# Conv layer of a diffusion step: opening by pairs of channel blocks, layer norm split in three parts

## The chip, the cores and the metric

The kernel runs on one core of a Trainium2 chip. The metric is the device time of one execution in microseconds (us), median of several runs. The core has a matrix engine (TensorE, in the profile PE, its weight loads PEld), a vector engine (VectorE, DVE), a scalar engine (ScalarE, ACT), GpSimd (POOL) and SyncE (SP), which here only issues DMAs. Each engine works through its own instruction list in order; engines are ordered among each other by semaphores alone, all written out by hand in this kernel.

## The reference, cut to what matters

One step of a two-layer backbone over T = 384 tokens: 128 context tokens (condition `c_ctx`) and 256 latent tokens (condition `c`). D = 1024, so there are 8 channel blocks of 128. Layer 0 mixes tokens with a convolution module; this case changes its opening and its layer norm. A dense SwiGLU, a latent attention layer and a mixture of 8 experts follow and are untouched.

```python
def adaln(cond, w, b):                       # w is D x 6D
    m = jax.nn.silu(cond) @ w + b
    return jnp.split(m[:, None, :], N_MOD, axis=-1)   # shift, scale, gate, shift, scale, gate

def conv_module(h, pw1, dw, dw_b, ln_g, ln_b, pw2):
    a, g = jnp.split(h @ pw1, 2, axis=-1)
    u = a * jax.nn.sigmoid(g)
    u = lax.conv_general_dilated(u, dw, ...31 taps, per channel...) + dw_b
    u = jax.nn.silu(layer_norm(u, ln_g, ln_b))
    return u @ pw2

# layer 0:  m = adaln(cond, ada_w[0], ada_b[0])
h = rms_norm(x, norm1_g[0]) * (1 + m[1]) + m[0]
x = x + m[2] * conv_module(h, ...)
```

## The kernel before, in words

**Weights.** All weights come through one ring of 6 slots of 1 MiB (`raw`, 128 x 2048 floats), numbered `s` and loaded by SP in that order; `load` makes SP wait until the chunk six places earlier has been read. Adaptive-norm chunks (`ada`) are used whole, in fp32: `cst` (the silu of both conditions, padded to 32 columns) is the stationary operand, four matmuls of 512 columns write four column groups of one PSUM bank, and eight chunks add up to one third of a layer's modulation. All other weights are split in two parts of lower width: ACT copies the chunk into `wh` (`make_hi`, L255), DVE subtracts it into `wl` (`make_lo`, L261), three buffers each (`HL`); a product is then three matmuls (`mm3`, L277 to L279). Activations are split the same way by DVE (`split_block`, L415 and L417).

**Opening.** SP loads three `ada` chunks, then x, then five more `ada` chunks; a chunk is 128 rows of ada_w, each 2048 columns and so 8 KB in one piece. These eight give shift and scale of the first norm for all channels. ACT squares x (L309), DVE takes the inverse root (`rsqrt`) and scales x into `xn` (L387), PE transposes `xn` block by block (`norm_pe`, L396). After the eighth chunk DVE adds the bias (`add_bias`, L1042), PE transposes the rows (`turn_rows`, L1650), DVE forms `modv` and `modA` (`modulation`), ACT applies them to each transposed block (L321), DVE splits it, and PE may start on it.

**Rounds.** `conv_pw1` comes in 8 chunks of 1 MiB (`PW1 + 3 r`; 1 KB pieces). Round r has 48 matmuls of 384 columns (two output blocks times 8 channel blocks times 3) and then two further `ada` chunks. Even rounds give two blocks of `a`, odd rounds the matching two of `g`; after each odd round ACT takes the sigmoid and DVE multiplies (`glu`, L1080). DVE carries the depthwise convolution of 6 of the 8 blocks, 31 taps each, 186 instructions (L1068, L1072); `ROUND_TAPS` says how many in which round, with `glu` and the `make_lo` of the next round's chunk ahead of them. ACT builds diagonal matrices (`diagonal`, L713), with which PE convolves the last two blocks after the rounds (L1697), between further `ada` chunks.

**Layer norm.** After the taps PE sums over channels with a matrix of ones (L1691), DVE centres the 8 blocks (L1123), ACT squares them, PE sums again (L1713). ACT takes one root over all 399 columns (L749), DVE one reciprocal (L1128), and then per block a scaling (L1132), a silu on ACT (L753) and the split. PE starts `conv_pw2` when block 0 is split for all tokens.

Of the kernel before, what the change touches and what calls it, by code (L numbers as in the profile page):

```python
# [53 lines left out]
def hybrid_conv_mla_diffusion_step(nc, d, out):  # L54
# [30 lines left out]
    PW1 = ADA_G  # L85
    ADA1 = PW1 + 3 * DK
# [20 lines left out]
    with ctx:  # L107
# [19 lines left out]
        vT = sb("vT", [P, 64])  # L127
# [62 lines left out]
        N1G, N2G, DWB, LNG, LNB, QNG, QKG, KKG = 0, 16, 32, 40, 48, 56, 62, 63  # L190
# [15 lines left out]
        kinds = [False] * ADA_G + [True, False, False] * DK + [False] * (2 * ADA_G) + [True] * 6 + [False] * DK  # L206
# [25 lines left out]

        def load(sp, s, src, view, loop=None):
# [16 lines left out]
        def make_hi(act, s, loop=None):  # L250

            turns = None if loop is None else (loop[0], loop[1] // RAW * 16)
            act.wait_ge(raw_in[s % RAW], at(16 * (s // RAW + 1), turns))
# [52 lines left out]
        def norm_act(act, q, layer, n, before_, count, banks=(6, 7) * 4, between=None, blocks=range(DK)):  # L306
# [8 lines left out]
            if layer == n == 0:  # L315
                make_hi(act, PW1)
            act.wait_ge(sem("mods"), 8 * layer + 4 * n + 4)
            for j in blocks:
                act.wait_ge(*of_norm(q, "turned", DK, j + 1))
# [7 lines left out]
        def norm_act_rows(act, q, layer, n, before_, banks, between=None):  # L327
# [16 lines left out]
            act.wait_ge(sem("mods"), 8 * layer + 4 * n + 4)  # L344
# [37 lines left out]
        def norm_dve(dve, step, q):  # L382
            dve.wait_ge(*of_norm(q, "squares", TC, TC))
            rsqrt(step, st[:, 4:4 + TC], st[:, 0:TC], TC)
            dve.sem_inc(sem("rstd"), 1)
            for c in (0, 2):
# [15 lines left out]
        CONV_BANKS = (2, 3, 6, 7, 0, 1, 6, 7)  # L402
        ADA_BANKS = ((5, 4), (6, 6), (7, 7), (2, 2), (6, 7), (0, 1))
        FFN_BANKS = (2, 3, 4, 5) * 2
        MODS_MADE = (4, 6, 8, 12, 14, 16)
# [6 lines left out]
        def split_block(dve, q, made, per, j):  # L412

            dve.wait_ge(sem(made), per * (j + 1))
# [16 lines left out]
        def _(sp):  # L431
# [5 lines left out]
            for n in range(ADA_G):  # L437
                if n == 3:
                    sp.dma_start(x[:, 0, :], d["x_prompt"][0]).then_inc(sem("x_in"), 16)
                    sp.dma_start(x[:, 1:3, :], d["x_sample"][0].rearrange("(c p) n -> p c n", p=P)).then_inc(sem("x_in"), 16)  # L440
                load_ada(n, 0, n)
            for r in range(DK):
                load(sp, PW1 + 3 * r, rows(d["conv_pw1"][0], 0, DK, r % 2 * D + r // 2 * 256, 256), as_rows(256, DK))
                for i in range(2):
                    load_ada(PW1 + 3 * r + 1 + i, 0, ADA_G + 2 * r + i)
# [94 lines left out]
        def _(pool):  # L540
# [8 lines left out]
            pool.memset(u[:, :, :], 0.0).then_inc(sem("zeroed"), 1)  # L549

            def fetch_bias(layer):
                b = d["ada_b"][layer].rearrange("(g j n) -> j g n", g=3, j=4)
                for j in range(4):
                    pool.dma_start(ab[32 * j:32 * j + 2, :, :], b[j].partition_broadcast(2)).then_inc(sem(f"bias_in{layer}"), 16)

            def keep_gate(layer, which):
                q = 3 * layer + 1 + which
                pool.wait_ge(sem("rows_added"), q + 1)
# [12 lines left out]
            fetch_bias(0)  # L571
# [3 lines left out]
            fetch_bias(1)  # L575
# [13 lines left out]
            pool.wait_ge(sem("mods"), 16)  # L589
# [101 lines left out]
        def _(act):  # L691
# [7 lines left out]
            for n, name in ((N1G, "norm1_g"), (N2G, "norm2_g"), (DWB, "conv_dw_b"), (LNG, "conv_ln_g"), (LNB, "conv_ln_b"),  # L699
                            (QNG, "mla_q_norm_g"), (QNG + 4, "mla_kv_norm_g")):  # L700
                vrow(n, d[name].rearrange("a (k p) -> (a k) p", p=P))
            vrow(QKG, d["mla_q_qk_g"][0:1, 0:P])
# [19 lines left out]
            for r in range(DK):  # L722
                if r + 1 < DK:
                    make_hi(act, PW1 + 3 * (r + 1))
                for n in range(3 * r, 3 * r + 3):
                    diagonal(n)
                if r % 2 == 1:
                    t = r // 2
                    act.wait_ge(chunk_used, used(PW1 + 3 * r))
# [1493 lines left out]
```

## Time and profile before

| | us |
|---|---|
| median of 3 runs | 1437.97 (1437.23 to 1440.47) |
| the profiled execution, its own time | 1436.74 |
| its span in the trace | 1435.0 |
| PE busy | 1366.1 |
| DVE busy | 1060.5 |
| ACT busy | 756.0 |
| DMA, mean over the span | 245 GB/s |

Span times run from the first instruction in the trace; 1.7 us lie around the span. PE is busy for 95% of it, but the share differs by stage, and the stages that the change touches are the first 238 us.

### The profile page before, as it was taken

Reading aid. Unit: us, or ns where it says so; the run is one execution under the profiler, and the core shown is the slowest. Engines: PE = TensorE matmul, PEld = TensorE weight load, DVE = VectorE, ACT = ScalarE, POOL = GpSimd, SP = SyncE. Lnnn points to the kernel's source line nnn. Section 1 sums busy time; section 2 is a strip of 40 time slices with the busy share of each in tenths; the row PEclk is TensorE's granted clock in tenths of the full one; section 3 lists DMA queues with packets and bytes.
Section 4 is the critical chain, followed back from the end, with each engine's and each line's share of the span. In section 5 each row is a group of like instructions: output and inputs, shape, how many; then the busy total and the mean of one; then the engine's idle time right before and its main releaser. Section 6 shows DMA issues by size and latency. Waiting matters only on the chain.

```text
span 1435.0 us, 18715 instructions
## 1 busy us (share of the span) xinstructions
PE 1366.1 (95%) x6686; PEld 1098.8 (77%) x6687; DVE 1060.5 (74%) x1328; ACT 756.0 (53%) x764; POOL 104.4 (7%) x129
## 2 busy tenths in 40 slices
PE   4999989999999989899999988999999999999997
PEld 1885457899999978677777766888878878778875
DVE  2589995443343447888888888888888888888986
ACT  2421354331322345655565545777777777777773
POOL 2000000401000000100000004500000000000003
PEclk8999999999999999999999998999999999999999
DMA  9898656999843323322212324999999999999994
GB/s 376 293 335 318 224 185 225 396 368 69 188 140 100 98 88 101 109 93 67 66 66 92 111 92 159 422 357 388 368 362 395 369 363 395 371 361 385 381 359 154
DMA packets 91914, 351.17 MB, mean 245 GB/s; under 512 B 7279, under 2 KB 43447, under 8 KB 62679
## 3 DMA queue, kind: packets, MB, share of 16 engines
q1 hardware_dynamic: 81088, 316.95, 61.7%
q0 software_dynamic: 9040, 28.66, 5.8%
q10 hardware_dynamic: 1735, 4.89, 0.9%
q8 instruction: 30, 0.49, 0.1%
q14 instruction: 21, 0.17, 0.0%
HBM read 326.13 MB, written 24.35 MB: 244 GB/s over the span
## 4 chain that ended last, share of the span: by engine, by line
PE 82%; DVE 8%; ACT 4%; issue 3%; DMA 2%; ACTq 0%; POOL 0%; DVEq 0%; POOLq 0%
PE ps L277 23%; PE ps L279 22%; PE ps L278 22%; PE ps L1697 3%; PE ps L1642 3%; DVE wl L261 2%; DVE hm L1549 2%; PE ps L1943 2%; PE ps L1974 2%; DMA raw<-in_conv_pw 1%; ACT wh L255 1%; PE ps L1947 1%; PE ps L2105 1%; PE ps L2064 1%; ACT QB L850 0%
## 5 line engine op out<-in xcount | busy, mean ns | idle before, releaser
L261 DVE TENSOR_TENSOR wl<-raw,wh 128x2048 fp32r<-128x2048 f32 x253 | 575.8, 2290 | 146.5 <-ACT wh L255 146.2
L255 ACT ACTIVATE wh<-raw 128x2048 fp32r<-128x2048 f32 x253 | 484.1, 1917 | 302.4 <-PE ps L279 260.4
L277 PE MATMUL ps<-wh,xgh 128*128 128x512 f32 x432 | 173.6, 402 | 0.2 <-DVE wl L261 0.2
L279 PE MATMUL ps<-wh,xgl 128*128 128x512 f32 x432 | 171.2, 396 | 0.0
L278 PE MATMUL ps<-wl,xgh 128*128 128x512 f32 x432 | 171.0, 396 | 0.0
L277 PE MATMUL ps<-hTh,wh 128*128 128x384 f32 x480 | 164.9, 344 | 1.8 <-DVE hTl L417 1.8
L278 PE MATMUL ps<-hTl,wh 128*128 128x384 f32 x480 | 163.5, 341 | 0.0
L279 PE MATMUL ps<-hTh,wl 128*128 128x384 f32 x480 | 163.2, 340 | 0.0
L277 PE MATMUL ps<-wh,hgh 128*128 128x512 f32 x288 | 116.3, 404 | 4.6 <-DVE hgl L1555 1.9
L279 PE MATMUL ps<-wh,hgl 128*128 128x512 f32 x288 | 114.1, 396 | 0.0
L278 PE MATMUL ps<-wl,hgh 128*128 128x512 f32 x288 | 114.1, 396 | 0.0
L1072 DVE SCALAR_TENSOR_TENSOR v<-u,dwT,v 128x399 f32<-128x399 f32 x180 | 99.0, 624 | 0.0
L277 PEld LDWEIGHTS ps<-hTh,wh 128*128 128x128 f32 x480 | 90.8, 189 | 10.5 <-issue 8.1
L279 PEld LDWEIGHTS ps<-wh,xgl 128*128 128x128 f32 x432 | 81.4, 188 | 19.8
L1156 DVE TENSOR_TENSOR ff<-ps,fs 128x384 f32<-128x384 f32 x22 | 12.3, 557 | 113.9 <-PE ps L279 113.9
L277 PEld LDWEIGHTS ps<-wh,xgh 128*128 128x128 f32 x432 | 81.4, 188 | 19.2 <-DVE wl L261 0.4
L278 PEld LDWEIGHTS ps<-wl,xgh 128*128 128x128 f32 x432 | 81.4, 188 | 18.2
L278 PEld LDWEIGHTS ps<-hTl,wh 128*128 128x128 f32 x480 | 90.8, 189 | 0.4
L279 PEld LDWEIGHTS ps<-hTh,wl 128*128 128x128 f32 x480 | 90.8, 189 | 0.0
L277 PEld LDWEIGHTS ps<-wh,hgh 128*128 128x128 f32 x288 | 54.2, 188 | 21.9 <-DVE wl L261 6.9
L279 PEld LDWEIGHTS ps<-wh,hgl 128*128 128x128 f32 x288 | 54.2, 188 | 13.1
L278 PEld LDWEIGHTS ps<-wl,hgh 128*128 128x128 f32 x288 | 54.3, 189 | 12.2
(368 smaller groups left out, 2127.4 us busy)
## 6 DMA issues: line engine op xcount, KB each, us to landing
raw<-in_moe_w SPq DMA_DIRECT2D x180, 1024.0 KB, 6.4
raw<-in_ada_w SPq DMA_DIRECT2D x48, 1024.0 KB, 7.2
raw<-in_ffn_w SPq DMA_DIRECT2D x33, 1024.0 KB, 12.1
raw<-in_conv_pw SPq DMA_DIRECT2D x12, 1024.0 KB, 9.2
raw<-in_mla_wo SPq DMA_DIRECT2D x8, 1024.0 KB, 4.9
xs_dram<-hf POOLq DMA_DIRECT2D x14, 512.0 KB, 21.4
ys_dram<-hf POOLq DMA_DIRECT2D x14, 512.0 KB, 22.4
raw<-in_mla_wuq SPq DMA_DIRECT2D x8, 768.0 KB, 4.6
```

The lines of the kernel that those rows point to most:

```text
L255: act.activation(wh[:, split_no(s) % HL, :], raw[:, s % RAW, :], ACT.Copy).then_inc(hi_made, 1)
L261: eng.tensor_tensor(wl[:, split_no(s) % HL, :], raw[:, s % RAW, :], wh[:, split_no(s) % HL, :], ALU.subtract).then_inc(lo_made, 1)
L277: nc.tensor.matmul(out_, sh, mh, start=start, stop=False)
L278: nc.tensor.matmul(out_, sh, ml, start=False, stop=False)
L279: return nc.tensor.matmul(out_, sl, mh, start=False, stop=stop)
L1072: dve.scalar_tensor_tensor(out=v[:, j, :], in0=u[:, j, w:w + CV], scalar=dwT[:, w * DK + j:w * DK + j + 1], in1=v[:, j, :], op0=ALU.mult, ...
L1549: dve.tensor_tensor(hm[:, g, :].rearrange("p (j r) -> p r j", j=4), ps[:, 3 + g, :].rearrange("p (r j) -> p r j", j=4), ms[:, g, :].rearra ...
L1642: last = pe.matmul(ps[32 * j:32 * j + 32, ADA_BANKS[q][0], :], cst[:, k, :], raw[:, s % RAW, j * 512:(j + 1) * 512], start=k == 0, stop=k ...
L1697: pe.matmul(ps[:, i, 0:CV], diag[:, m % DIAGS, :], u[:, DVE_BLOCKS + i, w:w + CV], start=w == 0, stop=w == CW - 1).then_inc(sem("diag_used ...
L1943: pe.matmul(ps[:, 2 * h + c // 2, a:b], QB[:, h, c * P:(c + 1) * P], KT[:, h, k0:k1], start=True, stop=False)
L1947: last = pe.matmul(ps[:, 2 * h + c // 2, a:b], QB[r0:r1, 2, c * P:(c + 1) * P], KR[r0:r1, k0:k1], start=False, stop=True)
L1974: last = pe.matmul(ps[:, 3 + h, P:T], v_sb[:, i, k + 1, h, :], pT[:, h, 2 * P * k:2 * P * (k + 1)], start=k == 0, stop=k == 2)
```

## The change

It does these things:

- The chunks that open the kernel are cut otherwise. An opening `ada` chunk now holds, for four row blocks of ada_w, 256 columns of shift and the 256 matching columns of scale, 1 KB pieces, loaded by two DMAs. Two such chunks (a pair) give shift and scale of two channel blocks for both conditions. The matmuls of one chunk write four row groups of a bank, each a partial sum; the four are added when the rows are turned, by a matmul against `folded_in`, a sum of four slices of the identity.
- Order of loads: x first, then pair 0, one `conv_pw1` chunk, pairs 1 and 2, one `conv_pw1` chunk, pair 3. The two `conv_pw1` chunks hold rows 0 to 511 and 512 to 1023 for two blocks of `a` and the two matching blocks of `g`; so the work of rounds 0 and 1 runs block by block (`open_block`, 12 matmuls each into four banks), two blocks per pair.
- The bias of this part comes transposed with the vectors (`ADB`, one more small DMA on ACT's queue).
- The 16 `ada` chunks of the rest of layer 0 lie in rounds 2 to 7: 3, 3, 3, 3, 2, 2 (before: two in each of 8 rounds). `add_bias(1)`, `turn_rows(1)` and `modulation(1)` come one round later.
- `ROUND_TAPS` has 78 taps in rounds 2 to 7, before 74.
- Layer norm: root, reciprocal, and for block 0 scaling, silu and split, run in three parts of 128, 143 and 128 columns; PE takes the first tokens of block 0 when the first part is split. `turn_rows(4)` comes after the second chunk of `conv_pw2`, before after the first.
- GpSimd fetches the bias for two thirds of layer 0 only and clears `u` after that.

```diff
+    QUARTERS = DK // 2
+    PAIR_BLOCKS = 4
+    OPEN = (0, 1, 3, 4, 5, 6, 8, 9)
+    ADA_ROUND = (0, 0, 3, 3, 3, 3, 2, 2)
+    PW1 = [2, 7] + [10 + r - 2 + sum(ADA_ROUND[:r]) for r in range(2, DK)]
-    ROUND_TAPS = (0, 0, 13, 13, 12, 12, 12, 12)
+    ROUND_TAPS = (0, 0, 14, 14, 13, 13, 12, 12)
+    LN_PARTS = ((0, P, 0), (P, SV + P, P), (SV + P, CV, 2 * P))
...
+            def load_pair(s, w, half, c0):
+                for t in range(2):
+                    load(sp, s, rows(w, 4 * half, 4, t * D + c0, 256),
+                         lambda slot: slot.rearrange("p (k t n) -> p k t n", k=4, t=2)[:, :, t, :])
...
+            def keep_rows(p):
+                dve.wait_ge(ada_used, 2 * (p + 1))
+                if p >= 2:
+                    dve.wait_ge(sem("rows_turned"), p - 1)
+                dve.tensor_copy(ar[:, p % 2, :], ps[:, p % 2, :]).then_inc(sem("rows_added"), 1)
...
-            norm_dve(dve, step, "conv")
+            norm_dve(dve, step, "conv", lambda: keep_rows(0))
...
+            modulation_pair(0)
+            for p in range(QUARTERS):
+                if p % 2 == 0:
+                    make_lo(dve, PW1[p // 2])
+                split_block(dve, "conv", "conv_modulated", 2, 2 * p)
+                split_block(dve, "conv", "conv_modulated", 2, 2 * p + 1)
+                if p + 1 < QUARTERS:
+                    keep_rows(p + 1)
+                    modulation_pair(p + 1)
...
+            ada_pair(0)
+            turn_vectors()
+            pe.wait_ge(sem("dw_made"), 3)
+            norm_pe(pe, "conv", CONV_BANKS, (0, 1))
+            turn_pair(0)
+            for p in range(QUARTERS):
+                if p + 1 < QUARTERS:
+                    ada_pair(p + 1, (0,))
+                    norm_pe(pe, "conv", CONV_BANKS, (2 * p + 2, 2 * p + 3))
+                if p % 2 == 0:
+                    wait_parts(pe, PW1[p // 2])
+                open_block(2 * p)
+                if p + 1 < QUARTERS:
+                    ada_pair(p + 1, (1,))
+                    turn_pair(p + 1)
+                open_block(2 * p + 1)
...
+            for i in range(TC + 1):
+                if i < TC:
+                    a, b, _ = LN_PARTS[i]
+                    dve.wait_ge(sem("ln_root"), i + 1)
+                    step(dve.reciprocal(rs[:, a:b], sd[:, a:b]))
+                else:
+                    dve.tensor_tensor(v[:, 1, :], v[:, 1, :], rs, ALU.mult).then_inc(sem("ln_scaled"), 1)
+                if i > 0:
+                    o = LN_PARTS[i - 1][2]
+                    dve.wait_ge(sem("ln_done"), i)
+                    high = dve.tensor_copy(hTh[:, 0, o:o + P], hf[:, 0, o:o + P])
...
+                    dve.tensor_tensor(hTl[:, 0, o:o + P], hf[:, 0, o:o + P], hTh[:, 0, o:o + P], ALU.subtract)\
+                        .then_inc(sem("ln_h_lo"), 1)
+                if i < TC:
+                    dve.tensor_tensor(v[:, 0, a:b], v[:, 0, a:b], rs[:, a:b], ALU.mult).then_inc(sem("ln_scaled"), 1)
```

## Rows read from the trace of the kernel before

**Rows 1.** Page, head and part 1: the span and the matrix engine's share.

```profile
span 1435.0 us, 18715 instructions
PE 1366.1 (95%) x6686; PEld 1098.8 (77%) x6687; DVE 1060.5 (74%) x1328; ACT 756.0 (53%) x764; POOL 104.4 (7%) x129
```

**Rows 2.** Stages: length, busy PE, PEld, DVE, ACT, POOL, PE clock, DMA share, GB/s.

```profile
0.00:37.00 37.00, 16.80 (x95) 5.58 (x96) 8.67 (x27) 11.46 (x20) 7.81 (x15) 0.83 0.97 375
60.40:124.00 63.60, 63.50 (x389) 53.29 (x389) 54.79 (x89) 16.43 (x26) 2.19 (x4) 1.00 0.85 314
124.00:187.50 63.50, 62.53 (x244) 28.01 (x244) 62.44 (x120) 16.87 (x42) 3.28 (x6) 1.00 0.66 233
187.50:201.70 14.20, 10.30 (x49) 3.31 (x49) 13.56 (x17) 9.49 (x16) 0.00 (x0) 1.00 0.51 173
```

**Rows 3.** Timeline of the opening: start, length, engine, line, operation, count [idle before].

```profile
15.93 1.06 ACT L309 ACTIVATE xn<-x 128x1024 f32<-128x1024 f32 x1 [8.21 <-DMA x<-in_x_sample]
18.45 1.93 PE L1642 MATMUL ps<-raw,cst 128*32 128x512 f32 x8 [6.26 <-DMA raw<-in_ada_w]
21.77 1.42 DVE L387 TENSOR_SCALAR xn<-x,st 128x1024 f32<-128x1024 f32 x2
30.22 0.69 DVE L1042 TENSOR_TENSOR ar<-ps,ab 128x512 f32<-128x512 f32 x1 [3.87 <-issue]
30.96 0.66 PE L1650 MATMUL ps<-ident,ar 128*128 128x128 f32 x4 [0.88 <-DVE ar L1042]
33.20 6.53 ACT L321 ACTIVATE hf<-ps,modv,modA 128x128 f32<-128x128 f32 x16
33.33 2.29 DVE L261 TENSOR_TENSOR wl<-raw,wh 128x2048 fp32r<-128x2048 f32 x1 [1.29 <-ACT wh L255]
35.53 0.35 DVE L415 CAST hTh<-hf 128x384 fp32r<-128x384 f32 x1
35.92 0.56 DVE L417 TENSOR_TENSOR hTl<-hf,hTh 128x384 fp32r<-128x384 f32 x1
```

**Rows 4.** Windows as in rows 2: first ada chunks moving, then a conv_pw1 chunk.

```profile
20.00:25.00 5.00, 3.90 (x20) 0.40 (x16) 2.76 (x11) 1.15 (x1) 0.00 (x0) 0.52 1.01 421
44.00:46.00 2.00, 2.00 (x13) 2.00 (x12) 1.34 (x1) 1.40 (x4) 0.00 (x0) 1.00 1.09 350
```

**Rows 5.** Chain of waits that ended last, two matmuls of 384 columns: start, length.

```profile
37.79 0.32 PE ps L278
42.66 0.18 PE ps L277
```

**Rows 6.** Timeline of rounds 1 to 3: adas of one round, a load, its copy, taps.

```profile
58.41 1.92 PE L1642 MATMUL ps<-raw,cst 128*32 128x512 f32 x16
60.83 0.38 SPq L240 DMA_DIRECT2D raw<-in_conv_pw  x1
70.37 1.92 ACT L255 ACTIVATE wh<-raw 128x2048 fp32r<-128x2048 f32 x1 [8.03 <-DMA raw<-in_conv_pw]
74.53 7.17 DVE L1072 SCALAR_TENSOR_TENSOR v<-u,dwT,v 128x399 f32<-128x399 f32 x13
```

**Rows 7.** Timeline: the last glu, and the last channel sum before the mean.

```profile
122.92 1.02 DVE L1080 TENSOR_TENSOR u<-ps,sg 128x256 f32<-128x256 f32 x2 [0.32 <-ACT sg L732]
186.49 0.51 PEld L1691 LDWEIGHTS ps<-v,ones 128*128 128x128 f32 x2 [0.16 <-DVE v L1072]
```

**Rows 8.** Timeline of the layer norm: root, reciprocal, silu, first matmul of conv_pw2.

```profile
195.68 0.59 ACT L749 ACTIVATE sg<-ps,epsc 128x399 f32<-128x399 f32 x1
196.31 2.65 DVE L1128 RECIPROCAL sg<-sg 128x399 f32<-128x399 f32 x1 [0.31 <-ACT sg L749]
199.60 3.62 ACT L753 ACTIVATE hf<-v,vT 128x128 f32<-128x128 f32 x8 [2.02 <-DVE v L1132]
201.72 0.47 PE L277 MATMUL ps<-wh,hTh 128*128 128x512 f32 x1 [3.65 <-DVE hTl L417]
```

**Rows 9.** Window as in rows 2: the matrix engine's clock after a wait.

```profile
35.00:36.00 1.00, 0.15 (x1) 0.18 (x2) 0.97 (x3) 1.00 (x4) 0.00 (x0) 0.50 0.94 352
```

More of the change, by code:

```diff
@@ L231, in ffn_chunk, with landed @@
             return GATE2 - 2 + n if n < 2 else FFN + n
+        def landed(s):
+            return 16 * (s // RAW + 1 + sum(o % RAW == s % RAW for o in range(min(s + 1, PW1[2]))))
         def load(sp, s, src, view, loop=None):
@@ L385, in norm_dve @@
             dve.sem_inc(sem("rstd"), 1)
+            between()
             for c in (0, 2):
@@ L1651, in turn_rows, with ada_pair @@
                 last.then_inc(sem("rows_turned"), 1)
-            for n in range(ADA_G):
-                ada(n, 0, n)
-                if n == 5:
-                    turn_vectors()
-                if n == 6:
-                    pe.wait_ge(sem("dw_made"), 3)
-                    norm_pe(pe, "conv", CONV_BANKS, range(6))
-            turn_rows(0)
-            norm_pe(pe, "conv", CONV_BANKS, range(6, DK))
-            for r in range(DK):
-                t, s = r // 2, PW1 + 3 * r
+            def ada_pair(p, halves=(0, 1)):
+                for half in halves:
+                    s = OPEN[2 * p + half]
+                    pe.wait_ge(raw_in[s % RAW], landed(s))
+                    for k in range(4):
+                        last = pe.matmul(ps[32 * k:32 * k + 32, p % 2, :], cst[:, 4 * half + k, :],
+                                         raw[:, s % RAW, k * 512:(k + 1) * 512], start=half == 0, stop=half == 1)
+                    last.then_inc(ada_used, 1)
@@ new lines, in turn_pair, with open_block @@
+            def turn_pair(p):
+                if p == 0:
+                    pe.wait_ge(sem("pair_fold"), 2)
+                pe.wait_ge(sem("rows_added"), p + 1)
+                for i in range(4):
+                    last = pe.matmul(ps[:, p % 2, 2 * i:2 * i + 2], ar[:, p % 2, i * P:(i + 1) * P], folded_in[:, :],
+                                     start=True, stop=True)
+                last.then_inc(sem("rows_turned"), 1)
+            def open_block(k):
+                pe.wait_ge(sem("conv_h_lo"), k + 1)
+                hi, lo = parts(PW1[k // 4], 512, 4)
+                for m in range(PAIR_BLOCKS):
+                    last = mm3(ps[:, 2 + m, 0:T], hi[:, k % 4, m * P:(m + 1) * P], lo[:, k % 4, m * P:(m + 1) * P],
+                               hTh[:, k, :], hTl[:, k, :], k == 0, k == DK - 1)
+                if k % 4 == 3:
+                    last.then_inc(chunk_used, 1)
@@ L1664, in _ @@
+            n_ada = ADA_G
+            for r in range(2, DK):
+                t, s = r // 2, PW1[r]
                 wait_parts(pe, s)
@@ L1677, in _ @@
                 last.then_inc(chunk_used, 1)
-                for i in range(2):
-                    ada(s + 1 + i, 0, ADA_G + 2 * r + i)
-                if r == 4:
+                for i in range(ADA_ROUND[r]):
+                    ada(s + 1 + i, 0, n_ada)
+                    n_ada += 1
+                if r == 5:
                     turn_rows(1)
@@ L1720, in pw2_block @@
                 k = 2 * q + i
-                pe.wait_ge(sem("ln_h_lo"), k + 1)
+                pe.wait_ge(sem("ln_h_lo"), c + 1 if k == 0 else TC + k)
                 for h in range(2):
```

158 lines of the change are left out of this document (89 added, 69 removed).

## The prediction

> **What bounds the kernel now.** I read the head of the page first: PE is busy for 95% of the span [rows 1], so a change can win only where PE is not busy, or is busy at its lower clock. Then I cut the first 238 us into stages with the view of windows [rows 2]. The reader should see four different things there. Up to 37 us PE is busy for less than half of the time and the DMA engines are full (share 0.97): the opening waits for bytes. From 60.4 to 124 (rounds 2 to 7) PE is busy all the time, DVE for 54.8 of 63.6 us. From 124 to 187.5 both are, 62.5 us each. From 187.5 to 201.7 PE lacks 3.9 us, while DVE is busy for 13.6 of 14.2: the layer norm waits for DVE. Whatever is won in one stage is kept only if DVE in the next can follow; that is the whole question here. The profiled execution took 1436.74 us, 1.2 below the median of 1437.97; I work with differences in its span and take them off the median.
>
> **Opening: when the bytes land.** The trace gives two rates: 421 GB/s while 8 KB pieces move, 350 GB/s while 1 KB pieces move [rows 4]. One MiB so takes 2.5 us in the one form and 3.0 us in the other. x landed at 15.9 us behind 3 MiB of chunks [rows 3]; 4.5 MiB at 2.5 us are 11.25, so 4.7 us lie before the stream and around it. The change puts x first (1.5 MiB, landed near 8.4) and makes all ten opening chunks of 1 KB pieces: chunk 0 lands at 11.4, chunk 1 at 14.4, then one each 3.0 us: the first conv_pw1 chunk (2) at 17.4, the last (9) at 38.4, the next conv_pw1 (10) at 41.4. Before, eight ada chunks and the first conv_pw1 chunk were there by 31.4. So the new order brings work earlier, but the whole of it later.
>
> The Trainium skill (DMA: Bandwidth & Descriptors, Specifications) states a minimum of 512 B for line rate. By that rule the 1 KB pieces would lose nothing and the result would be the small rival named below; the trace speaks against it.
>
> **Opening: the first block.** DVE has the norm's inverse root ready before 14.4, but the change then makes it wait in `keep_rows(0)` for pair 0, and the scaling of x (1.4 us, [rows 3]) is queued behind that wait, and behind that the copies of the vectors, the transposes on PE and the turn. With an ada chunk at the low clock (1.9 us for one, [rows 3]): pair done 16.3; kept 17.0 (0.69, as the bias addition); x scaled 18.5; vectors copied 19.1 (0.6, three small copies); blocks 0 and 1 transposed and the pair turned by 21.3 (0.3 to 0.66 for a turn, [rows 3]); modulation of the pair 0.6, so 21.9. Then DVE makes `wl` (2.2 in sequence) and splits block 0 (0.9 for both steps) [rows 3]: PE's first `open_block` starts near 25.0. Before, the first matmul of this kind came at 37.1.
>
> **Opening: the pace.** An `open_block` is 12 matmuls of 0.18 us, 2.1 us at the full clock, 3.8 us at the lower (0.32 each, [rows 5]). Per pair PE does two of them (4.2), two ada chunks (0.95 each, [rows 6]), six transposes (0.8), and in `turn_pair` it waits for `keep_rows`, for which DVE needs 0.75 with the hop, plus 0.4 for the turn itself. That is 8.2 us a pair against 7.5 us of DMA (two and a half chunks), so with these terms PE's own chain sets the pace. From 25.0: block 0, an ada chunk, keep, turn and block 1 are 6.4; two full pairs 16.4; the last two blocks 4.2: rounds 0 and 1 are done at 52.0. Round 2 needs the `wl` of chunk 10, for which ACT starts only when all eight blocks are split: the last split comes about 3.6 us after the last turn (45.7), then 1.9 and 2.3 us of hi and lo: **round 2 starts at 53.0 to 53.6**, taken as 53.0 (hops between engines could add half a microsecond). Before it started at 60.4 [rows 2, 6]. So 7.4 us are won at this point. The bounds: 47.7 if only the landing of chunk 9 counted (38.4, then 9.3 us from ada to `wl`), and 57 if blocks 0 and 1 and what lies between ran at the lower clock and every hop cost 0.2 more. Folding four partial sums costs four tiny matmuls in place of four transposes, nothing measurable; what hides the two extra DMA issues per chunk (0.38 each, [rows 6]) is the 3.0 us that a chunk needs.
>
> **Rounds: what is given back.** The four ada chunks that lay in rounds 0 and 1 now lie in rounds 2 to 5: 4 x 0.95 = 3.8 us on PE, which is busy there throughout. Round 7's matmuls end at 53.0 + 51 + 14 x 0.95 + 1 = 118.3, before 121.9. DVE is the nearer limit. In round r it must make the `wl` of chunk r+1 ahead of its taps, and that chunk comes later now: with four chunks a round and six slots, SP may load conv_pw1 chunk r+2 only when the second ada chunk of round r has been read. Before, its issue at 60.83 hung on round 1 for chunk 4, and ACT copied it from 70.4 on [rows 6]. Now chunk 4 hangs on round 2: matmuls done at 61.5, first ada read at 62.4, two chunks of 2.5 and 3.0 plus 2.4 us of latency (the 60.83 load with two ada chunks 1.3 us ahead of it needed 10.5 for 8.1 us of bytes), landed 70.4, copied 72.4. So DVE starts round 3's taps at nearly the same time as before, whatever was won ahead. From there: 72.4 + 2.2, 14 taps (0.545 each in a series, [rows 6]), glu 0.95; chunk 5 is copied one PE round (11.35) after chunk 4, at 83.8; + 2.2 + 13 taps; chunk 6 at 95.1; + 2.2, bias 0.6, 13 taps, glu, `wl` 2.2, 12 taps, 12 taps: DVE is through at **121.4**, against PE's 118.3. The last glu so starts at 121.4, before at 122.92 [rows 7]: **1.5 us of the 7.4 are left.** Loads for three-ada rounds fill 10.5 to 10.7 of 11.35 us; the `wl` for PE is ready 1.0 us before PE wants it.
>
> **After the rounds.** PE is bound by its diagonals and ada chunks and DVE by its taps, and they meet at 186.5, where PE waits 0.16 and just before it 0.29 us for taps [rows 7]. DVE has four taps less (2.2 us), PE nothing less: **0.4 us.**
>
> **Layer norm.** Now root 195.7, reciprocal to 199.0, scaling, silu, split, PE at 201.7 [rows 8]. In three parts: first root 0.35 us, reciprocal 2.65 x 128/399 plus a fixed part = 0.95, scaling 0.3: 197.35. ACT does two more roots and reloads its table (1.3) until 198.1, silu 0.45, DVE cast and subtraction 0.5: PE starts at 199.15. Part 2 is split at 200.9, part 3 at 202.15, block 1 at 204.0 (before about 202.9), then one block each 1.35 us against 4.2 on PE. At the full clock PE does each third in 1.4 us, waits a little, and stands at 204.0 for block 1; seven blocks of 4.23 and the rest as before end at 234.0, before 237.5. **3.5 us.** At the lower clock, as now in the first 4 us, it would be 2.6, which is the lower bound; the upper is 4.0. I take 3.5 because PE's pause shrinks from 3.65 to 1.1 us. `turn_rows(4)` keeps its 0.4 us; what waits behind `modulation(4)` on DVE is the `wl` of the fourth conv_pw2 chunk, ready near 220 and wanted at 225.
>
> **Sum.** 1.5 + 0.4 + 3.5 = 5.4 us. After 238 us PE is the bound again and everything shifts. 1437.97 - 5.4 = 1432.6.
>
> **Rivals.** First, *the opening runs at the pace of its bytes*: round 2 at 47.7, DVE through at 116.1; gain 6.8 + 0.4 + 3.5 = 10.7, 1427.3. For it speaks the full DMA share [rows 2], against it the 8.2 us chain a pair. Second, *late conv_pw1 chunks*: the loads of three-ada rounds have 6% of air. If each lands 2 us later than computed, PE loses 1 us every second round and DVE 3 us by the end; its 1.5 becomes -1.5: gain 2.4, 1435.6. For it: before, chunk 7 came late while the gate fetch shared the engines. Third, on the other side, *the clock stays low through the opening*. After its 4.2 us pause PE's clock stood at the lower level [rows 9], and stayed there until 41.7. The new opening has a pause before every turn and before block 0. Four blocks at the lower clock cost 4 x 1.7 us, the ada chunks and transposes among them 5: 12 us later, 1444.6. It decides the sign once more than 5.4 us are lost, about half of that stretch. Against it: from 19 us on PE's pauses are each under 1.5 us.
>
> Two small ones shift the first block. *Block 0 at the lower clock*: before it lie mostly transposes and pauses, and before this change the clock rose only 4.6 us after the first matmul of the block kind; 1.7 us more, 1434.3. The Trainium skill (TensorE: Matmul & The Clock Gate, Part 4) says that transposes do not count as activity for the clock, which is this case; the trace can't separate it. *1 KB pieces at 421 GB/s*: chunks 0 and 1 each land 0.5 us earlier, the end 1.0: 1431.6; the 350 GB/s of [rows 4] are against it. This is what the 512 B of the Trainium skill's DMA page would give.
>
> **Chances.** Forecast 0.36, block 0 at the lower clock 0.11, 1 KB pieces at full rate 0.04, bytes' pace 0.12, late chunks 0.25, low clock 0.09, something else 0.03. 2.9 us are 0.2%, about what a measurement of this kernel can tell from no change. Faster by more (below 1435.1): the forecast and the small ones nearly whole (0.46 of 0.51), bytes' pace, a quarter of the late chunks, 0.64. Within: 0.26. Slower: 0.10. The range takes in the first two rivals and the bounds of the layer norm: 1427 to 1438.5.
>
> **What would show it.** Opening right: first open matmul near 25, round 2 near 53, the clock at 2.4 GHz from block 1 on. Rounds: DVE idle for about 7.5 us before the `wl` of chunk 4 near 72, then PE waiting for the last glu near 121 to 122 (about 2.5 us). Layer norm: first conv_pw2 matmul 2.9 us after the first reciprocal's start (now 5.4), at the full clock. Wrong: a round 2 before 50 or after 56, or a wait of PE for `wl` in rounds 3 to 6.

## The result and the profile after

The changed kernel took 1424.47 us (median of four, 1421.14 to 1427.03), the kernel before 1437.65 in the runs beside it. The ratio is 0.9903, with a 95% interval of 0.9885 to 0.9922: 13.2 us faster. The forecast was 5.4 us faster, 1432.6, in a range of 1427.0 to 1438.5; the time lies 2.5 us below that range.

The profiled execution took 1427.03 us. Page, head and part 1, after, beside [rows 1]:

```profile
span 1425.3 us, 18840 instructions
PE 1356.0 (95%) x6715; PEld 1097.1 (77%) x6715; DVE 1064.8 (75%) x1350; ACT 756.0 (53%) x767; POOL 102.9 (7%) x129
```

The share of PE is the same 95%, but its sum fell by 10.1 us, with no fewer matmuls. That is the first hint: a change that removes waits shortens the span and leaves the sum. A window of 100 us late in the kernel, where the change touches no instruction, says it plainly (length, then busy time and count of PE, PEld, DVE, ACT, POOL, clock, DMA share, GB/s). Before:

```profile
1000.00:1100.00 100.00, 99.73 (x447) 80.16 (x446) 88.09 (x48) 72.77 (x45) 0.00 (x0) 1.00 0.96 372
```

After:

```profile
1000.00:1100.00 100.00, 99.40 (x454) 80.86 (x453) 89.14 (x49) 74.32 (x47) 0.00 (x0) 1.00 0.97 381
```

Both at the full clock, both with PE busy throughout, and 454 matmuls in place of 447. The timeline of PE at 1000 us shows the pace of single matmuls (start, length). Before:

```profile
999.99 0.40 PE L277 MATMUL ps<-wh,xgh 128*128 128x512 f32 x1
1000.22 0.39 PE L278 MATMUL ps<-wl,xgh 128*128 128x512 f32 x1
1000.46 0.39 PE L279 MATMUL ps<-wh,xgl 128*128 128x512 f32 x1
1000.69 0.40 PE L277 MATMUL ps<-wh,xgh 128*128 128x512 f32 x1
```

After:

```profile
999.91 0.39 PE L287 MATMUL ps<-wh,xgh 128*128 128x512 f32 x1
1000.14 0.39 PE L288 MATMUL ps<-wl,xgh 128*128 128x512 f32 x1
1000.37 0.39 PE L289 MATMUL ps<-wh,xgl 128*128 128x512 f32 x1
1000.59 0.39 PE L287 MATMUL ps<-wh,xgh 128*128 128x512 f32 x1
```

Three matmuls need 0.70 us before and 0.68 after. Lengths overlap and are rounded, so from here on I use the mean distance from start to start of neighbouring matmuls of one kind over the whole trace, called the *spacing*; distances above 0.26 us (0.2 us for 384 columns), where PE did or waited for something else, are left out. For the expert products (2160 matmuls: three rows of 432 and three of 288 in the groups by line) it is 234.1 ns before and 229.3 after. 2160 x 4.8 ns are 10.4 us.

What the forecast spoke of lies in the first 235 us. Timeline of PE after, the opening:

```profile
14.20 1.93 PE L1730 MATMUL ps<-raw,cst 128*32 128x512 f32 x8 [1.14 <-DMA raw<-in_ada_w]
18.81 1.54 PE L407 MATMUL ps<-ident,xn 128*128 128x128 f32 x6 [1.93 <-DVE vT L1137]
25.60 0.66 PE L287 MATMUL ps<-hTh,wh 128*128 128x384 f32 x1 [0.42 <-DVE hTl L428]
26.06 0.52 PE L288 MATMUL ps<-hTl,wh 128*128 128x384 f32 x1
26.38 0.52 PE L289 MATMUL ps<-hTh,wl 128*128 128x384 f32 x1
...
29.71 1.07 PE L1730 MATMUL ps<-raw,cst 128*32 128x512 f32 x8
31.61 1.05 PE L1740 MATMUL ps<-folded_in,ar 128*128 128x2 f32 x8 [0.82 <-DVE ar L1093]
32.52 0.42 PE L287 MATMUL ps<-hTh,wh 128*128 128x384 f32 x1
...
50.46 0.42 PE L287 MATMUL ps<-hTh,wh 128*128 128x384 f32 x1
...
58.34 0.44 PE L287 MATMUL ps<-hTh,wh 128*128 128x384 f32 x1 [0.78 <-DVE wl L271]
```

Block 0 starts at 25.60, but its matmuls stand 0.32 us apart, the pace of the lower clock in [rows 5]; from 32.5 on they stand 0.18 apart. The clock column of the windows does not show this:

```profile
25.60:29.60 4.00, 4.00 (x12) 3.67 (x12) 0.68 (x2) 0.00 (x0) 0.00 (x0) 1.00 1.10 349
```

It reads 1.00 from the start of this trace to 128.8 us. So the lower clock of block 0 is read from the distance of the matmuls alone. The row at 58.34 is round 2 (before, the same kind of row starts at 60.27; the prediction took 60.4).

Timeline after, from the fourth conv_pw1 chunk's issue to the first diagonals (answering [rows 6, 7]):

```profile
68.91 0.38 SPq L250 DMA_DIRECT2D raw<-in_conv_pw  x1
77.97 2.29 DVE L271 TENSOR_TENSOR wl<-raw,wh 128x2048 fp32r<-128x2048 f32 x1 [8.09 <-ACT wh L265]
126.67 1.01 DVE L1126 TENSOR_TENSOR u<-ps,sg 128x256 f32<-128x256 f32 x2
127.74 3.39 PE L1806 MATMUL ps<-u,diag 128*128 128x399 f32 x6 [2.72 <-DVE u L1126]
```

And the layer norm after (answering [rows 8]):

```profile
193.06 3.93 DVE L1178 SCALAR_TENSOR_TENSOR v<-ps,v 128x399 f32<-128x399 f32 x8 [5.17 <-PE ps L1800]
201.53 0.95 DVE L1187 RECIPROCAL sg<-sg 128x128 f32<-128x128 f32 x1 [0.15 <-ACT sg L774]
204.57 0.47 PE L287 MATMUL ps<-wh,hTh 128*128 128x512 f32 x1 [1.12 <-DVE hTl L1199]
```

The wait of PE before conv_pw2 fell from 3.65 to 1.12 us. Behind it the clock stays full, where before it stood at 0.50 from 202.3 on:

```profile
202.30:205.70 3.40, 3.40 (x10) 2.63 (x9) 3.30 (x9) 2.82 (x7) 0.00 (x0) 0.50 1.10 351
```

Yet the first row of the conv layer's last step comes late. Timeline of DVE, before:

```profile
233.47 1.22 DVE L364 TENSOR_TENSOR xn<-ps,gate 128x1024 f32<-128x1024 f32 x1
```

After:

```profile
234.87 1.22 DVE L374 TENSOR_TENSOR xn<-ps,gate 128x1024 f32<-128x1024 f32 x1
```

I call this row the *end of conv*. From it to the end of the span the kernel before needs 1201.5 us and the changed one 1190.4. So the part that was rebuilt lost 1.4 us in these executions, and the part in which no instruction differs won 11.1.

### The profile page after: what moved, and what is told of

It is laid out like the page before. It is cut to its first block, busy times and chain, and to the rows that moved or that the text cites. A ratio compares the mean times of both kernels' runs of the same rounds, so it can differ in the third digit from the quotient of the medians.

```text
span 1425.3 us, 18840 instructions
## 1 busy us (share of the span) xinstructions
PE 1356.0 (95%) x6715; PEld 1097.1 (77%) x6715; DVE 1064.8 (75%) x1350; ACT 756.0 (53%) x767; POOL 102.9 (7%) x129
## 4 chain that ended last, share of the span: by engine, by line
PE 73%; DVE 11%; DMA 5%; ACT 4%; issue 4%; DVEq 0%; POOL 0%; ACTq 0%; SPq 0%; POOLq 0%
PE ps L287 20%; PE ps L289 19%; PE ps L288 19%; DMA raw<-in_ffn_w 3%; PE ps L1806 3%; DVE wl L271 3%; PE ps L1713 2%; DVE hm L1622 2%; PE ps L2052 2%; ACT wh L265 2%; PE ps L2083 2%; DVE v L1118 1%; PE ps L2056 1%; PE ps L2214 1%; PE ps L2173 1%
## 5 line engine op out<-in xcount | busy, mean ns | idle before, releaser
L288 PEld LDWEIGHTS ps<-wl,hgh 128*128 128x128 f32 x288 | 54.1, 188 | 11.1
```

The costliest lines, as they stand in the source:

```text
L288: nc.tensor.matmul(out_, sh, ml, start=False, stop=False)
```

## The experiments

**What could make untouched matmuls faster.** The full diff has one edit that reaches them (the excerpt above leaves it out): `vT` grows from 64 to 80 columns (64 bytes of each partition) and `folded_in`, 2 columns, comes behind it. Every tile allocated later moves, among them `hTh`, `xgh`, `hgh`, `ckTh`, `fh`, `oTh`; `raw`, `wh` and `wl` lie ahead of it and stay. In an expert product the moving operand is `wh` or `wl` and the stationary one `xgh` or `xgl`; in conv_pw1 `hTh` is moving and `wh` stationary. The theory: this move alone makes the gain. The rival: the gain comes from the new instructions (another rhythm of DMAs or of the clock after the conv layer).

The first set crosses the two. `e1_before_shifted` moves the tiles of the kernel before:

```diff
         vT = sb("vT", [P, 64])
+        spare = sb("spare", [P, 16])
+        spare2 = sb("spare2", [P, 2])
```

> The kernel before, with only two unused tiles of 16 and 2 columns put behind vT, so that every tile allocated after it lies where the changed kernel has it; no instruction differs. In the two traces the first 240 us of the changed kernel end 1.4 us later (first xn<-ps,gate at 234.87 against 233.47), and yet it is 13 us faster: the matmuls of 512 columns follow each other every 229.3 ns instead of 234.1. Theory A (the tiles' place in memory sets that spacing): this kernel is at about 1427, with 229 ns. Theory B (the spacing comes from what the new opening or layer norm does to the engines' timing or clock): it stays at 1437 to 1438 with 234 ns.

Measured: 1424.32 us, ratio 0.9899 (0.9883 to 0.9916), spacing 229.2 ns. The clock is not what made it faster: the granted clock as a mean over the profiled execution was 0.981, and 0.982 in that of the kernel before. The same window of 100 us:

```profile
1000.00:1100.00 100.00, 99.43 (x454) 81.05 (x453) 89.19 (x49) 74.21 (x47) 0.00 (x0) 1.00 0.97 382
```

The move acts on the conv layer too: the end of conv comes at 230.85 in e1, 2.6 us earlier than before.

`e2_after_unshifted` is the opposite, the changed kernel with its tiles back:

```diff
-        vT = sb("vT", [P, 80])
-        folded_in = sb("folded_in", [P, 2])
+        spare = sb("spare", [P, 64])
...
+        vT = sb("vT", [P, 80])
+        folded_in = sb("folded_in", [P, 2])
```

> The changed kernel, with vT and folded_in allocated behind all other tiles and an unused tile of 64 columns in the old place of vT: all other tiles lie as in the kernel before. Theory A: about 1438 to 1439 us, spacing 234 ns, so that the change without the shift of memory is 1 us slower than before. Theory B: stays at 1424, 229 ns.

Measured: 1438.59 us, 0.9995 (0.9977 to 1.0014), spacing 234.1. Its window of 100 us has the old count again:

```profile
1000.00:1100.00 100.00, 99.74 (x447) 80.12 (x446) 87.99 (x49) 72.30 (x45) 0.00 (x0) 1.00 0.96 374
```

Two unused tiles give the whole of the change's gain; without the move, all of its new instructions together give nothing that can be measured. `e3_after_old_norm` takes the changed kernel with the layer norm of before, `e4_before_new_norm` the kernel before with the new layer norm:

```diff
-            act.activation(sd, ps[:, 5, 0:CV], ACT.Sqrt, ...).then_inc(sem("ln_root"), 1)
+            for a, b, _ in LN_PARTS:
+                act.activation(sd[:, a:b], ps[:, 5, a:b], ACT.Sqrt, ...).then_inc(sem("ln_root"), 1)
...
```

> The changed kernel with the layer norm in one piece as before and turn_rows(4) in its old place; the new opening stays. Between the centring (5.4 us late) and the end of conv_pw2 (1.4 us late) the changed kernel won 4.0 us, so: 4.0 us slower than the changed kernel, about 1428.5, and conv_pw2's first matmul about 6.4 us after the last channel sum instead of 3.9. A rival: the 4 us come from the clock, which did not fall at conv_pw2, for a reason that is not the shorter pause; then the first matmul comes 2.5 us later and the clock does not fall: 2.6 us slower.

> The kernel before with only the layer norm in three parts and turn_rows(4) moved. My forecast's term was 3.5 us (2.6 to 4.0), the traces say 4.0: 1433.6 to 1434.2, at the spacing of before (234 ns), since no tile moves by it. If the layer norm had to do with the spacing, it would be at 229 ns and some 9 us faster still.

Measured: 1430.43 us, 0.9939 (0.9922 to 0.9956), and 1433.72 us, 0.9961 (0.9947 to 0.9975). By the medians the norm is worth 6.0 us in the changed kernel and 5.1 in the kernel before (by the ratios 5.2 and 5.6), within their uncertainty one number. The trace of e4 puts 3.7 us of it before the end of conv (229.81 against 233.47), where it was meant to be, and that of e3 3.6 (238.47 against 234.87): 2.5 by the shorter wait and the rest by the clock. Timeline of e3's PE, and the window behind it, for comparison with the row at 204.57 above:

```profile
207.11 0.77 PE L286 MATMUL ps<-wh,hTh 128*128 128x512 f32 x1 [3.65 <-DVE hTl L427]
207.10:210.50 3.40, 3.39 (x8) 2.72 (x9) 3.30 (x9) 2.81 (x7) 0.00 (x0) 0.50 1.10 359
```

So e3's rival falls. In all 14 traces with the old norm PE waits some 3.65 us here, and the clock drops to 0.50 behind it in 13 of them (not in f1, below); in the 6 with the new norm (wait 1.1 us) it drops in none.

The same set prices the new opening. e2 is e4 plus the opening, and e3 is e1 plus the opening: it makes the kernel 4.9 us slower in the one pair and 6.1 in the other.

**Which move.** The next kernels are the kernel before with unused tiles of other sizes or at other places; no instruction differs in any of them. `f1_before_shift64` has 16 columns behind `vT`, `f2_before_shift256` 64, and `f3_before_shift128_all` 32 columns ahead of `raw`, so that `wh` and `wl` move too. `f4_before_norm_shifted` is e4 with the tiles of e1.

> The kernel before with one unused tile of 16 columns (64 bytes a partition) behind vT. Moving all tiles behind vT by the 16 + 2 columns of the change gave 229 ns instead of 234 ns for every 512-column matmul, 14 us. Theory A1: the spacing depends on where the stationary operand lies against a boundary of 256 bytes or so, and 64 bytes off it count as badly as 128: 234 ns, 1438. Theory A2: any other place than that of before is better: 229 ns, 1424.

> As before, with an unused tile of 64 columns (256 bytes) behind vT. Theory A1, a period of 256 bytes or less: the same as before, 234 ns and 1438. If the distance between the operands or a longer period counts: 229 ns and 1424.

> As before, with an unused tile of 32 columns (128 bytes) ahead of the first tile, so that both operands of every matmul move by the same. If the distance between stationary operand (behind vT) and moving operand (wh, wl, ahead of it) sets the spacing: as before, 234 ns, 1438. If the place of the stationary operand alone does: 229 ns, 1424. If the moving operand counts too, anything, also above 234.

> The kernel before with its old opening, the layer norm in three parts, and the unused tiles of 16 and 2 columns behind vT: what helped, without what did not. Old opening 5.4 us earlier at the centring than the new one: 1424.3 (shift alone) minus 4 to 5 (the norm's effect alone) = 1419.5 to 1420.5, and 4 to 5 us faster than the changed kernel. If the gains do not add, it stays at the changed kernel's 1424.

Measured: f1 1434.98 us, 0.9983 (0.9972 to 0.9993); f2 1438.44, 1.0004 (0.9992 to 1.0017); f3 1437.84, 0.999 (0.9976 to 1.0003); f4 **1419.28**, 0.987 (0.9848 to 0.9891). f4 is faster than both kernels (its slowest execution, 1420.80, lies below the fastest of the changed kernel, 1421.14): it keeps the norm and the move and leaves the new opening out.

So not every move helps, and both theories of f1 fell: its spacing is 233.3, between them. The next four ask for amount and place: `g1_before_shift128` (32 columns behind `vT`), `g2_before_shift2cols` (2 columns there), `g3_before_1618_all` (the tiles of e1, but ahead of `raw`) and `g4_before_1618_later`, the tiles of e1 further back, between the group that holds `hTh`, `xgh`, `hgh`, `ckTh` and the groups that hold `fh` and `oTh`:

```diff
             [("rows_pad", [P, 28, P], F32), ("router", [P, DK, NE], F32), ...
+        spare = sb("spare", [P, 16])
+        spare2 = sb("spare2", [P, 2])
         (xn,), (v,), (k_sb, v_sb) = share(
```

> The kernel before with one unused tile of 32 columns, 128 bytes, behind vT. Found so far: 16 + 2 columns behind vT give 229 ns; 16 columns 233 ns; 64 columns 234 ns; 32 columns ahead of all tiles 234 ns. If the two unused tiles of the fast kernel take 64 bytes each (tiles begin at multiples of 64), this one is the same shift: 229 ns, 1424. If tiles begin at multiples of 32 or less, the fast shift was 96 or 72 bytes, and this one is a new place: theory A3, a period of 128 bytes, gives 234 ns, 1437.

> As before with an unused tile of 2 columns (8 bytes, or what a tile's start is rounded to). If tiles begin at multiples of 64, the same shift as the 16 columns: 233 ns, about 1435. If at multiples of 32: a shift by 32 bytes, not measured yet; by theory A3 (period of 128 bytes, best place 96) it should be worse than 96, so 230 to 234 ns.

> The two unused tiles of 16 and 2 columns ahead of the first tile: both operands of each matmul move. If the place of the stationary operand counts by itself: 229 ns, 1424. If the distance between the operands counts: 234 ns, 1437.

> The two unused tiles of 16 and 2 columns behind the shared group that holds hTh, hTl, xgh, hgh and ckTh, so that those stay where they are in the kernel before, while oTh and fh (and all vector data behind) move. If the stationary operand's place counts: 234 ns where xgh, hgh or ckTh is stationary, 229 where oTh or fh is; in time some 1.5 us less than before, 1435.5. If it is a matter of what the other engines read and write (hm, ms, ff, u, v): 229 ns everywhere, 1424.

Measured: g1 1431.72 us, 0.9953 (0.9935 to 0.9971); g2 1434.4, 0.997 (0.9957 to 0.9984); g3 1436.94, 0.9997 (0.9987 to 1.0008); g4 1438.28, 1.0001 (0.999 to 1.0012). g1 met neither of its theories, with a spacing of 233.2 and a time between the two. In total g4 is a miss. The two kinds that became faster should save some 3 us, but its profiled execution stood 7 us longer at the lower clock behind the end of conv (34.2 against 27.2 us), which takes about as much; whether that is so in the median isn't shown. Its spacings settle the place:

| spacing, ns, by the activation operand | before | e1 | g3 | g4 |
|---|---|---|---|---|
| xgh, hgh (experts) | 234.1 | 229.2 | 234.1 | 234.2 |
| ckTh | 234.3 | 229.1 | 234.2 | 234.2 |
| fh | 234.0 | 229.5 | 234.0 | 229.2 |
| oTh | 234.0 | 229.7 | 233.9 | 229.5 |

Only the kinds whose own tile moved against `wh` and `wl` became faster; moving both operands alike does nothing. So it is a distance that counts, not where a tile lies by itself. I take it to be the distance between the two operands of a matmul. `raw`, `x` and `ident` lie ahead of `vT` as well and kept their distance to `wh` and `wl` in all these kernels; a tile between `raw` and `wh`, which would tell them apart, was not tried.

The last ones sweep the amount behind `vT`: `h3_before_shift24cols`, `h4_before_shift8cols`, `i1_before_shift56cols`, `i2_before_shift40cols`:

```diff
         vT = sb("vT", [P, 64])
+        spare = sb("spare", [P, 24])
```

> The kernel before with one unused tile of 24 columns (96 bytes) behind vT. If tiles begin at multiples of 32 bytes, the fast shift (tiles of 16 and 2 columns) was 96 bytes: 229 ns and 1424. If they begin at multiples of 8 or 4, it was 72 bytes and this is a new place: between 229 and 234 ns.

> The kernel before with one unused tile of 8 columns (32 bytes) behind vT. If tiles begin at multiples of 32 bytes, this is the same as the tile of 2 columns: 232.8 ns (384 columns: 176), 1434.4. If they do not, a new place.

> The kernel before with one unused tile of 56 columns (224 bytes) behind vT; no instruction differs. If the pattern repeats every 128 bytes, 224 is like 96: 229.2 ns between 512-column matmuls and a total near 1423 us (ratio 0.990). If 96 bytes is a single fast place, 233 ns or more and 1432 to 1438 us. I hold the repeat more likely, at 0.6, though 0 and 128 bytes (234.1 and 233.2) are not quite alike.

> The kernel before with one unused tile of 40 columns (160 bytes) behind vT; no instruction differs. If the pattern repeats every 128 bytes, 160 is like 32: 232.8 ns and near 1435 us (0.998). If it is not periodic, nothing says what it gives; at 229 ns and 1423 us it would show that the fast distances lie elsewhere than at 96 plus multiples of 128.

All amounts together. The last two columns have 384 moving columns: `hTh` is moving and `wh` stationary (conv_pw1 and the products of this form behind it), while with `cqTh` the roles are as in the experts.

| kernel | columns, bytes | us | ratio (95%) | experts, ns | hTh, ns | cqTh, ns |
|---|---|---|---|---|---|---|
| before | 0 | 1437 | 1 | 234.1 | 176.7 | 174.3 |
| g2 | 2, 8 | 1434.40 | 0.997 (0.9957 to 0.9984) | 233.0 | 176.0 | 176.2 |
| h4 | 8, 32 | 1435.29 | 0.998 (0.9968 to 0.9992) | 232.7 | 176.0 | 176.2 |
| f1 | 16, 64 | 1434.98 | 0.9983 (0.9972 to 0.9993) | 233.3 | 174.5 | 176.6 |
| h3 | 24, 96 | 1422.59 | 0.9893 (0.9873 to 0.9913) | 229.2 | 174.8 | 173.3 |
| e1 | 16 and 2, 72 | 1424.32 | 0.9899 (0.9883 to 0.9916) | 229.2 | 174.4 | 173.3 |
| g1 | 32, 128 | 1431.72 | 0.9953 (0.9935 to 0.9971) | 233.2 | 173.6 | 176.5 |
| i2 | 40, 160 | **1418.41** | 0.9864 (0.9838 to 0.989) | 227.6 | 173.7 | 174.0 |
| i1 | 56, 224 | 1430.84 | 0.995 (0.9933 to 0.9967) | 233.2 | 173.4 | 173.5 |
| f2 | 64, 256 | 1438.44 | 1.0004 (0.9992 to 1.0017) | 234.1 | 176.7 | 174.3 |

Rows g2 and h4 agree within 0.3 ns, and e1 and h3. That fits tiles whose size counts in steps of 32 bytes, so that 16 and 2 columns are 96 bytes. Both expectations of the last two kernels fell: I held it likely that the pattern repeats every 128 bytes, and then 224 should have been fast and 160 slow. It is the other way round. The eight amounts are in keeping with a pattern that repeats after 256 bytes and is fast at 96 and 160, next to the half of it, and not at the half itself; between 160 and 224, and beyond 256, nothing was run. The amounts are counted from the kernel before, whose own distance is not 0. Added up from the sizes in the kernel in steps of 32 bytes, its activation tiles lie 96 bytes past a multiple of 256 from `wh`, and so those of i2 would lie at a multiple of 256; this is an estimate, no run read an address. i2 is the fastest kernel of all that were run, with not one instruction changed. Its window of 100 us:

```profile
1000.00:1100.00 100.00, 99.23 (x455) 81.28 (x454) 89.47 (x49) 74.33 (x47) 0.00 (x0) 1.00 0.97 381
```

**What the new opening loses.** Two kernels change the opening of the changed kernel. `h2_after_warm` puts 16 matmuls of 128 columns, whose result nobody reads, into two of PE's waits before block 0 (5.5 and 1.9 us in the changed kernel), to raise the clock; `h1_after_ada_223333` moves two ada chunks from rounds 2 and 3 to rounds 6 and 7, so that the fourth conv_pw1 chunk comes earlier.

```diff
             pe.wait_ge(sem("cst_made"), 1)
+            busy(10)
             ada_pair(0)
             turn_vectors()
+            busy(6)
```

> The changed kernel with 16 idle matmuls (identity times ones, 128 columns, into a bank nobody reads) on PE: 10 ahead of pair 0, 6 behind the transposed vectors, where PE waits. In the changed kernel block 0 runs at the lower clock (0.32 us a matmul from 25.6 to 29.7). If the clock is what costs it, block 0 takes 2.1 instead of 3.8 us and round 2 starts 1.5 to 2.5 us before 58.3; all later loads hang on it, so the total falls by as much: 1422 to 1423. If the landing of the chunks or DVE's chain paces the opening, round 2 stays at 58.3 and the total at 1424.5.

```diff
-    ADA_ROUND = (0, 0, 3, 3, 3, 3, 2, 2)
+    ADA_ROUND = (0, 0, 2, 2, 3, 3, 3, 3)
```

> The changed kernel with its 16 later ada chunks placed 2, 2, 3, 3, 3, 3 over rounds 2 to 7 (changed: 3, 3, 3, 3, 2, 2), and add_bias(1), turn_rows(1), modulation(1) one round later, since the eighth of them now comes with round 5. Theory: in the changed kernel DVE waits 8.1 us (69.9 to 78.0) for the copy of conv_pw1 chunk 4, because SP may load that chunk only after the second ada chunk of round 2 is read (issue at 68.9). Here chunk 4 sits in the ring where chunk 10 of the opening was, free at 58.3, so the wait goes, the last glu comes at PE's pace near 124.2 instead of 126.7, PE's pause there and the fall of its clock at 129 go too: 4 us less, 1420.5. Rival: DVE's wait only moves to a later chunk (the loads of four 3-ada rounds come late instead), and it stays at 1424.

h2 took 1423.65 us, 0.9904 (0.9888 to 0.9921). Timeline of its PE:

```profile
23.53 0.41 PE L287 MATMUL ps<-hTh,wh 128*128 128x384 f32 x1 [0.85 <-DVE hTl L428]
23.78 0.34 PE L288 MATMUL ps<-hTl,wh 128*128 128x384 f32 x1
23.96 0.34 PE L289 MATMUL ps<-hTh,wl 128*128 128x384 f32 x1
...
54.38 0.45 PE L287 MATMUL ps<-hTh,wh 128*128 128x384 f32 x1 [0.83 <-DVE wl L271]
```

Block 0 runs at the full clock's pace of 0.18 us, 2.1 us earlier, and round 2 starts 4.0 us earlier than in the changed kernel, for 16 idle matmuls. That is more than the 1.5 to 2.5 expected. The end of conv comes at 229.89 in its trace, 5.0 us earlier. In the time of the runs only 0.8 us of this appear, less than they can tell. The two traces are not alike in luck either: that of the changed kernel is from its slowest execution of four (1427.03) and has the fall of the clock described below, that of h2 is from its fastest (1422.08) and has none.

h1 took 1424.64 us, 0.9903 (0.9887 to 0.992). Timeline of its DVE:

```profile
84.92 2.29 DVE L271 TENSOR_TENSOR wl<-raw,wh 128x2048 fp32r<-128x2048 f32 x1 [5.04 <-ACT wh L265]
...
98.04 2.29 DVE L271 TENSOR_TENSOR wl<-raw,wh 128x2048 fp32r<-128x2048 f32 x1 [3.74 <-ACT wh L265]
...
125.43 1.03 DVE L1126 TENSOR_TENSOR u<-ps,sg 128x256 f32<-128x256 f32 x2
```

The wait of 8.09 us for chunk 4 is gone, and waits of 5.04 and 3.74 us for chunks 5 and 6 have come. The last glu is 1.2 us earlier (125.43 against 126.67), of 2.5 expected, and in total there is nothing. The wait mostly moved, as the rival had it, and the clock fell behind the last glu here too.

## Why the prediction was wrong

Landmarks of five traces give the account; each is the start of a row of the kind shown above.

| | before | e2 | after | h2 | e4 |
|---|---|---|---|---|---|
| tiles moved by 96 bytes | no | no | yes | yes | no |
| round 2 | 60.27 | 57.44 | 58.34 | 54.38 | 60.14 |
| last glu | 122.92 | 125.76 | 126.67 | 123.32 | 122.79 |
| centring | 187.68 | 190.51 | 193.06 | 188.07 | 187.55 |
| conv_pw2 | 201.72 | 202.02 | 204.57 | 199.58 | 199.06 |
| end of conv | 233.47 | 232.77 | 234.87 | 229.89 | 229.81 |
| rest of the span | 1201.5 | 1201.3 | 1190.4 | 1190.4 | 1203.3 |

**The term that was missing.** The prediction says "After 238 us PE is the bound again and everything shifts". That is the step that failed, and its size decides the result: after the end of conv PE was the bound, but not at the same pace. The rest of the span fell by 11.1 us (before to after) and by 0.2 without the move (before to e2). I costed every instruction that the diff adds, and not the two lines that add none but place all others. The full diff has them (`vT`, `folded_in`); the trace of before could not have priced them.

**Opening, bytes.** Right. 1 KB pieces move at 348 GB/s in the window from 14 to 20 us, as [rows 4] said, and PE started on the two chunks of the first pair at 11.12 and 14.20, forecast 11.4 and 14.4. The rival of 421 GB/s is out, and with it what the minimum of 512 B in the Trainium skill (DMA: Bandwidth & Descriptors, Specifications) would have given.

**Opening, block 0.** Its start, forecast near 25.0, was 25.60. Its pace was the small rival: 0.32 us a matmul for all twelve, 4.0 us in place of 2.1, with ada chunks, transposes and waits before it. In e2 the pace rose in the middle of the block, in h2 before it, after idle matmuls. The Trainium skill (TensorE: Matmul & The Clock Gate, Part 4) has it that transposes do not count as activity. These rows don't contradict that, but no run shows it: h2 filled waits and kept every transpose.

**Opening, pace.** The forecast was too fast in three places. From the start of block 0 to the first turn's end I had 4.3 us and the trace has 6.9: 1.9 from the clock, most of the rest from the turn. The four matmuls of 2 columns in the code are eight in the trace (the row at 31.61) and take 0.9 us from their start to the next block, not the 0.4 I gave the turn, with matmuls called "tiny". A full pair so needs 8.97 us (32.52 to 41.51, 50.46), not 8.2: two of them 1.5 us. Together with 0.6 for the start and 0.6 behind the last turn, round 2 came at 58.3, not 53.0. Of these last 0.6, 0.5 were an error of addition: the prediction's own terms (3.6, 1.9 and 2.3 behind 45.7) give 53.5. Of the 7.4 us to be won there, 1.9 were.

**Rounds.** The model was right in form and size: last glu at round 2 + 68.4; measured 68.33 (after), 68.32 (e2), 68.94 (h2). DVE waits 8.09 us for chunk 4 and PE waits 2.72 for the last glu, as I had written (7.5 and about 2.5). But the model has the last glu hang on round 2 with no slack, so all that the opening missed came out here: 122.92 became 126.67, and the forecast gain of 1.5 us a loss of 3.8 (2.8 in e2).

**After the rounds.** 0.4 us were forecast, none came. From last glu to centring it is 64.76 us before, 64.75 in e2 and 64.75 in h2: PE sets this stretch, and four taps less only let DVE idle longer before the centring (1.24 us before, 3.52 in e2). In the profiled execution of the changed kernel it is 66.39, for a reason of its own. Windows of that stretch, after:

```profile
126.00:133.00 7.00, 5.26 (x15) 1.85 (x16) 7.00 (x14) 1.21 (x3) 3.29 (x6) 0.76 0.72 290
```

The clock is at 0.76 of the full one as a mean. Behind its wait for the glu PE needs 3.39 us for six matmuls with diagonals; in h2 the same six need 2.28:

```profile
124.39 2.28 PE L1812 MATMUL ps<-u,diag 128*128 128x399 f32 x6 [2.71 <-DVE u L1126]
```

h2 has the same wait, 2.71 us against 2.72, and keeps its clock; so does e2 (2.32). In e3 and h1 the clock fell after waits of only 2.59 and 2.02 us. So the length of the wait does not decide; what does stays open. The fall costs 1.6 us where it happens: from last glu to centring all three traces with the fall have 66.4 us.

**Layer norm.** Right to a tenth. With the tiles of before, centring to conv_pw2 is 14.04 us before and 11.51 in e4, and conv_pw2 to end of conv 31.75 and 30.75: 3.5 us, the forecast. First reciprocal to first matmul is 3.04 us, forecast 2.9, and the clock stayed full. The runs of e4 and e3 put 5 to 6 us on it, a little more than the traces do; their uncertainty of some 2 us each covers that.

**The sum again.** Without the move: -2.8 + 0 + 3.5 = 0.7 us won at the end of conv, as e2's trace shows, and 0.9995 in the ratio. So that the kernel became faster, as forecast, is luck: nothing that the prediction counts made it so. With the move: 13 to 14 us more. Of the rivals, "block 0 at the lower clock" came true, at a higher price than its 1.7 us since nothing behind it had slack; the bytes' pace and the late chunks did not, for PE waited for no `wl` in rounds 3 to 6. Had I sized the opening rightly, I should have forecast "the same", and been further off: the range could hold the result only with a term for memory places.

## What to carry to other kernels

Before a gain or loss of about 1% is put down to the instructions of a change, compare a stretch that the change doesn't touch: if the spacing of the same matmuls differs there, the placement of tiles has moved, and one kernel with an unused tile in place of the edit tells the two apart. In a kernel bound by fp32 matmuls, sweep the distance between the tiles of the two operands in steps of 32 bytes over 256; it costs one line and was worth 1.4% here. Take the parts of a change apart as well: here the norm won 5 to 6 us and the opening lost as much, and together they gave nothing. And cost every instruction of a new chain that has no slack, the small ones above all: a turn by matmuls of two columns took 0.9 us in place of 0.4, and a pair took 8.97 us in place of 8.2.

## What was not expected of the hardware

- The spacing of a matmul with 512 moving columns, written in the split fp32 form, depends on where the tiles lie to each other in SBUF, most likely on the distance between its stationary and its moving operand: 227.6 to 234.1 ns, 2.8%, at the same granted clock of 1.00 and with PE always busy. The Trainium skill (SBUF — State Buffer, Who interferes with whom) gives PE two independent read ports, for moving operand and weight load; that alone would leave no room for an effect of the distance, and the runs show one. Why it is so stays open: that the two reads collide is only a guess, and no run here looked at it.
- For 384 columns the order is another one, and it depends on the roles: with `hTh` moving 176.7 ns at 0 and 256 bytes and 173.4 to 173.7 at 128, 160 and 224; with `cqTh` stationary, the roles of the experts, 173.3 to 174.3 at 0, 96, 160, 224 and 256 and 176.2 to 176.6 at 32, 64 and 128. So the best distance for one product need not be that of another.
- With sixteen idle matmuls in two waits ahead of it a block ran at 0.18 us a matmul that had run at 0.32 without them, the paces of the full and the lower clock (2.4 and 1.2 GHz), and round 2 came 4.0 us earlier. How much of this stays in the median was not resolved.
- A wait of PE of 2.7 us was followed by a fall of the clock in one execution and not in another, and one of 2.0 us was followed by a fall too.
- i2 (40 columns) and the norm of e4 were not run together. If they add as e1 and e4 did in f4 (1424.32 and 1433.72 gave 1419.28), the two would be faster than either; that is an estimate, not a measurement.
